# Two changes to a two-block transformer kernel: the order of the last products of each FFN, and a shared weighted sum for the late modulation

## The chip, the cores and the metric

The kernel runs on one core of a Trainium2 chip. Its engines are TensorE (PE, matmuls; PEld is its loading of weights), VectorE (DVE), ScalarE (ACT), GpSimd (POOL) and SyncE (SP, which only issues DMAs here). The metric is the device time of one execution in microseconds. The kernel before takes 3024.43 us (median of 3 runs, 3019.88 to 3027.5). Lower is better.

## The reference

Two transformer blocks with 512 tokens and 1024 channels, all in float32. Two parts matter here. The first is the modulation of the first block (adaLN): a vector `mod` of 6 x 1024 numbers is computed from the condition `c`, and the last four sixths of it are needed only after the first mixer (the "late" part):

```
mod = jax.nn.silu(c) @ w_ada[l] + b_ada[l]
sh1, sc1, gt1, sh2, sc2, gt2 = [m[:, None, :] for m in jnp.split(mod, 6, axis=-1)]
...
x = x + gt1 * mixed
h2 = rms_norm(x, g_norm2[l]) * (1.0 + sc2) + sh2
```

The second is the FFN with a convolution over the tokens, which stands once in each of the two layers of the second block:

```
def _conv_ffn(x, w_up, conv_w, conv_b, w_down):
    g, u = jnp.split(x @ w_up, 2, axis=-1)
    gp = jnp.pad(g, ((0, 0), (half, half), (0, 0)))
    gc = conv_b
    for j in range(FFN_CONV):                    # FFN_CONV = 3
        gc = gc + conv_w[j] * gp[:, j:j + s]
    act = jax.nn.gelu(gc, approximate=False)
    return (act * u) @ w_down                    # inner width 2816
```

## The kernel before, in words

**Data.** Activations are held transposed: 128 channels on the partitions, 512 tokens along the free axis, 8 such tiles (`xT`). Weights come from memory in chunks of up to 128 x 2048 numbers. SyncE loads chunk k into `stage[k % 2]` once chunk k-2 has been split (semaphore `w_split`). ScalarE copies it to a rounded `wH` (line 312), VectorE subtracts to get the rest `wL` (line 317); there are four slots of `wH`/`wL`. Every product of the form weights times activations is three matmuls on TensorE: low x high, high x low, high x high (lines 347, 350, 351).

**The order of work** is written out by hand: each engine has its own program, and semaphores tie them together. Nothing reorders it.

**Late modulation (lines 1057 to 1090 on VectorE, 1745 to 1763 on TensorE).** While the retention of the first mixer is computed in 16 steps w (scores on TensorE, the decay product on VectorE in line 1080, line 1741 on TensorE), each step also handles one 1 MB chunk of `w_ada`, of two halves of 128 x 1024. VectorE multiplies each half by a number per partition and adds it to `ada_sum` (line 1064 for the first of a group, else line 1066). The chunks r and r+2 share a stage buffer: SyncE issues the load of r+2 once r is summed (line 428). After each group of four chunks TensorE sums over the partitions, by 8 matmuls of `ada_sum` with a column of ones (`late_mod`, line 1669 in the helper `mod_cols`; the profile counts 2 passes for each of these float32 matmuls). VectorE may overwrite `ada_sum` only when that is done (line 1059). The fourth result comes before the retention's group norm on TensorE (line 1766). GpSimd has no work in this stretch.

**FFN (lines 1466 to 1522 on VectorE, 814 to 840 on ScalarE, 1991 to 2023 on TensorE).** The inner width is 22 slabs of 128. For slab s TensorE computes the up product (gate and value, 16 x 3 matmuls), VectorE scales, convolves (lines 1495 to 1500), ScalarE applies gelu (line 826), VectorE multiplies (line 1504), ScalarE rounds to `faH` (line 830), VectorE forms `faL` (line 1506). Then TensorE computes the down product of that slab: 8 pieces of 3 matmuls, each into one of 4 PSUM banks in turn, and VectorE adds each piece to `xT` (line 1473) before the bank can be used again. TensorE's order is up(s), down(s-1), for s from 1 to 21, then down(21) alone. After FFN 0 comes the norm `mix1`, after FFN 1 the norm `final2`; each norm is a square on ScalarE (line 531) and a sum over partitions on TensorE (line 1652) for each of the 8 tiles.

## Time and profile before

| What | us |
|---|---|
| median of 3 runs | 3024.43 |
| the profiled execution | 3020.32 |
| its span, first to last instruction | 3018.5 |
| TensorE matmul busy | 2724.8 (90%) |
| VectorE busy | 2260.3 (75%) |
| ScalarE busy | 972.9 (32%) |
| GpSimd busy | 391.2 (13%) |

The late modulation lies between 220 and 295 us of the span, FFN 0 from about 1905 to 2272 us and FFN 1 from about 2635 to 2997 us. A row of a timeline gives the start, the duration, the engine, the line of the kernel, the operation, output <- inputs, the shape and the count; in brackets, how long the engine was idle before it and what released it. "issue" there means that the profile shows nothing that was waited for. PEclk, or the clock, is the share of the full TensorE clock (2.4 GHz) that was granted; 0.50 is 1.2 GHz.

### The profile page before, as it was taken

What the parts mean: (1) busy time and instruction counts of PE and PEld (TensorE: products, weight loads), DVE (VectorE), ACT (ScalarE), POOL (GpSimd) and SP (SyncE); (2) the same over time, 40 slices, a digit from 0 to 9 for tenths busy, and PEclk for the clock granted to TensorE, in tenths of its full rate; (3) what the DMA queues carried; (4) which work ended last, traced back from release to release, by engine and by line L of the source; (5) the groups of instructions that cost most, each with busy time, mean ns of one, the idle gap of its engine ahead of it and who ended that gap; (6) DMA issues with size and microseconds to landing.
All of it is one profiled execution on the core that took longest, in us unless ns stands there. A gap on an engine that the chain in (4) does not pass through costs nothing.

```text
span 3018.5 us, 38456 instructions
## 1 busy us (share of the span) xinstructions
PE 2724.8 (90%) x13529; PEld 2317.3 (77%) x13529; DVE 2260.3 (75%) x3559; ACT 972.9 (32%) x1266; POOL 391.2 (13%) x275
## 2 busy tenths in 40 slices
PE   2976778997999999899999994999999987999997
PEld 1763346897999999899999992788877842788885
DVE  5447755999899977688888877778776465478876
ACT  3220343343344433333333322222223254322221
POOL 0000100012222235333333330000000000000000
PEclk7986799999999999999999997999999998999998
DMA  5216001246788889889999981123222200122221
GB/s 207 91 49 240 32 15 58 84 156 230 245 300 301 299 322 380 326 314 346 347 345 350 344 291 37 65 89 104 87 94 84 98 15 1 49 100 95 99 88 56
DMA packets 158887, 515.47 MB, mean 171 GB/s; under 512 B 11729, under 2 KB 77649, under 8 KB 127057
## 3 DMA queue, kind: packets, MB, share of 16 engines
q1 hardware_dynamic: 109696, 326.62, 30.9%
q0 software_dynamic: 36864, 134.23, 12.2%
q10 hardware_dynamic: 12240, 53.48, 4.4%
q8 instruction: 52, 0.85, 0.1%
q14 instruction: 35, 0.28, 0.0%
HBM read 461.86 MB, written 52.43 MB: 170 GB/s over the span
## 4 chain that ended last, share of the span: by engine, by line
PE 74%; DVE 17%; DMA 4%; ACT 2%; issue 2%; POOL 0%; SPq 0%; ACTq 0%; DVEq 0%
PE ps L347 21%; PE ps L351 21%; PE ps L350 21%; PE ps L1901 3%; DVE sb_wL L317 2%; PE ps L1652 2%; DMA sb_rows<-u_rows,sb_row_at 1%; PE ps L2083 1%; DVE sb_stats L1576 1%; DMA sb_stage<-w_ada_l 1%; DVE sb_rows L1203 1%; DVE sb_ada_sum L1066 1%; PE ps L1835 1%; PE ps L1669 1%; DMA sb_xT<-x_l 1%
## 5 line engine op out<-in xcount | busy, mean ns | idle before, releaser
L347 PE MATMUL ps<-sb_hL,sb_wH 128*128 128x512 f32 (+1 forms) x2256 | 847.4, 376 | 91.0 <-DVE sb_wL L317 33.5
L351 PE MATMUL ps<-sb_hH,sb_wH 128*128 128x512 f32 (+1 forms) x2256 | 829.2, 368 | 0.0
L350 PE MATMUL ps<-sb_hH,sb_wL 128*128 128x512 f32 (+1 forms) x2256 | 828.6, 367 | 0.0
L317 DVE TENSOR_TENSOR sb_wL<-sb_stage,sb_wH 128x2048 fp32r<-128x2048 f32 (+2 forms) x257 | 539.1, 2099 | 188.4 <-ACT sb_wH L312 187.4
L312 ACT ACTIVATE sb_wH<-sb_stage 128x2048 fp32r<-128x2048 f32 (+2 forms) x257 | 447.4, 1758 | 335.3 <-PE ps L347 192.6
L347 PEld LDWEIGHTS ps<-sb_hL,sb_wH 128*128 128x128 f32 x2256 | 427.9, 190 | 155.3 <-issue 70.5
L350 PEld LDWEIGHTS ps<-sb_hH,sb_wL 128*128 128x128 f32 x2256 | 428.1, 190 | 54.1 <-issue 5.8
L351 PEld LDWEIGHTS ps<-sb_hH,sb_wH 128*128 128x128 f32 x2256 | 427.3, 189 | 51.1
L347 PE MATMUL ps<-sb_waL,sb_wH 128*128 128x384 f32 x1024 | 347.2, 339 | 19.2 <-issue 9.8
L351 PE MATMUL ps<-sb_waH,sb_wH 128*128 128x384 f32 x1024 | 346.6, 338 | 0.0
L350 PE MATMUL ps<-sb_waH,sb_wL 128*128 128x384 f32 x1024 | 346.6, 338 | 0.0
L1635 POOL DMA_INDIRECT sb_rows<-u_rows,sb_row_at x128 | 184.0, 1437 | 740.7 <-DVE sb_rows L1203 381.3
L1473 DVE TENSOR_TENSOR sb_xT<-sb_xT,ps 128x512 f32<-128x512 f32 x352 | 230.7, 683 | 39.3 <-PE ps L351 39.2
L1635 POOL DMA_INDIRECT sb_rows<-v_rows,sb_row_at x128 | 187.2, 1462 | 360.6 <-DVE sb_tok L1210 337.7
L347 PEld LDWEIGHTS ps<-sb_waL,sb_wH 128*128 128x128 f32 x1024 | 194.7, 190 | 20.2 <-DVE sb_waL L1362 10.1
L350 PEld LDWEIGHTS ps<-sb_waH,sb_wL 128*128 128x128 f32 x1024 | 194.6, 190 | 0.0
L351 PEld LDWEIGHTS ps<-sb_waH,sb_wH 128*128 128x128 f32 x1024 | 194.4, 190 | 0.0
L826 ACT ACTIVATE sb_gel<-sb_gcv 128x512 f32<-128x512 f32 x44 | 27.8, 632 | 489.9 <-DVE sb_gcv L1498 489.9
L1203 DVE SCALAR_TENSOR_TENSOR sb_rows<-sb_rows,sb_tok 128x1024 f32<-128x1024 f32 x128 | 152.2, 1219 | 36.8 <-DMA sb_rows<-u_rows,sb_row_at 36.7
L1210 DVE SCALAR_TENSOR_TENSOR sb_tok<-sb_rows,sb_row_act,sb_tok 128x1024 f32<-128x1024 f32 x128 | 164.0, 1281 | 10.9 <-DVE sb_tok L1210 2.3
L347 PE MATMUL ps<-sb_faL,sb_wH 128*128 128x512 f32 x352 | 140.8, 400 | 12.8 <-issue 12.8
L351 PE MATMUL ps<-sb_faH,sb_wH 128*128 128x512 f32 x352 | 139.6, 397 | 0.0
(334 smaller groups left out, 3245.2 us busy)
## 6 DMA issues: line engine op xcount, KB each, us to landing
sb_stage<-u_l SPq DMA_DIRECT2D x64, 1024.0 KB
sb_stage<-v_l SPq DMA_DIRECT2D x64, 1024.0 KB
sb_stage<-up_l SPq DMA_DIRECT2D x44, 1024.0 KB
g_scratch<-sb_ga ACTq DMA_DIRECT2D x64, 384.0 KB
w_scratch<-sb_wst ACTq DMA_DIRECT2D x12, 2048.0 KB, 9.9
sb_wg<-w_scratch SPq DMA_DIRECT2D x32, 768.0 KB
...
```

The source lines that it names most:

```text
L312: act.activation(wH[k % SLOTS][:, 0:n], stage[k % STAGES][:, 0:n], ACT.Copy).then_inc(w_hi, 1)
L317: dve.tensor_tensor(wL[k % SLOTS][:, 0:n], stage[k % STAGES][:, 0:n], wH[k % SLOTS][:, 0:n], ALU.subtract).then_inc(w_split, 1)
L347: m = pe.matmul(dst, lh, rl, start=first, stop=False)
L350: pe.matmul(dst, ll, rh, start=False, stop=False)
L351: return pe.matmul(dst, lh, rh, start=False, stop=last)
L1066: op = dve.scalar_tensor_tensor(ada_sum[:, :], w, sc[:, k:k + 1], ada_sum[:, :], ALU.mult, ALU.add)
L1203: dve.scalar_tensor_tensor(rows[r % 4][:, :], rows[r % 4][:, :], 1.0, tok[:, :], ALU.mult, ALU.mult, accum_out=column(row_act, r, i, per)) ...
L1210: dve.scalar_tensor_tensor(tok[:, :], rows[r % 4][:, :], column(row_act, r, i, per), tok[:, :], ALU.mult, ALU.add).then_inc(s_g["used"], 1)
L1473: dve.tensor_tensor(xT[:, d, :], xT[:, d, :], ps[:, 4 + d % 4, :], ALU.add).then_inc(s["added"], 1)
L1635: pool.indirect_dma_start(rows[r % 4][:, :], None, A["u_rows" if r < ROUNDS else "v_rows"], bass.IndirectOffsetOnAxis(ap=row_at[:, r % ROU ...
L1652: pe.matmul(ps[:, norm_bank(name), :], tab[:, ONES, :], scr[:, k % 2, :], start=k == 0, stop=k == nkt - 1).then_inc(s["sum"], 1)
L1901: m = pe.matmul(ps[:, 4 + g0 % 4, q * P:(q + 1) * P], oneJ[g0 % 4][:, q, :], oneI[g0 % 4][:, q, :], start=True, stop=True)
```

## The change

**Late modulation.** VectorE now handles only the first half of each chunk, into `ada_sum[0]`: one instruction in place of two. GpSimd handles the second half, into `ada_sum[1]`. From the second chunk of a group on it does so in two instructions: the half is multiplied in place, and then added. TensorE reduces both sums, with two matmuls per column in place of one. The load of chunk r+2 waits for both engines. Lines of the changed kernel are up to 50 higher.

What VectorE has in a row at the start of the loop, before:

```order
L1066 SCALAR_TENSOR_TENSOR sb_ada_sum<-sb_stage,sb_small,sb_ada_sum 128x1024 [waits ada_summed]
L1080 TENSOR_TENSOR sb_scr<-ps,sb_decay 128x384 [waits ret_ld0,ret_scores,ada_summed]
...
L1066 SCALAR_TENSOR_TENSOR sb_ada_sum<-sb_stage,sb_small,sb_ada_sum 128x1024 [waits ld_ada1]
L1066 SCALAR_TENSOR_TENSOR sb_ada_sum<-sb_stage,sb_small,sb_ada_sum 128x1024 [waits ada_summed]
L1080 TENSOR_TENSOR sb_scr<-ps,sb_decay 128x256 [waits ret_scores,ret_ld0,ret_y,ada_summed]
```

And after, on VectorE:

```order
L1090 TENSOR_TENSOR sb_scr<-ps,sb_decay 128x384 [waits ret_ld0,ret_scores,ada_summed]
L1090 TENSOR_TENSOR sb_scr<-ps,sb_decay 128x384 [waits ret_ld1,ret_scores]
L1076 SCALAR_TENSOR_TENSOR sb_ada_sum<-sb_stage,sb_small,sb_ada_sum 128x1024 [waits ld_ada1]
L1090 TENSOR_TENSOR sb_scr<-ps,sb_decay 128x256 [waits ret_scores,ret_ld0,ret_y,ada_summed]
L1090 TENSOR_TENSOR sb_scr<-ps,sb_decay 128x256 [waits ret_ld1,ret_scores]
```

The second `ada_sum` instruction of each chunk is gone there. GpSimd, which had nothing before its first `hL` subtraction, now has 28 instructions ahead of it, of which the first five are (the first of each group waits for TensorE's reduction of the group before, semaphore `ada_cols`; `ada_sum3` is `ada_sum[1]`):

```order
L1652 TENSOR_SCALAR sb_ada_sum3<-sb_stage0,sb_small 128x1024 [waits ada_cols,ld_ada0]
L1654 TENSOR_SCALAR sb_stage1<-sb_stage1,sb_small 128x1024 [waits ld_ada1,ada_halved]
L1656 TENSOR_TENSOR sb_ada_sum3<-sb_ada_sum3,sb_stage1 128x1024 [waits ada_bit]
L1654 TENSOR_SCALAR sb_stage0<-sb_stage0,sb_small 128x1024 [waits ld_ada0,ada_halved]
L1656 TENSOR_TENSOR sb_ada_sum3<-sb_ada_sum3,sb_stage0 128x1024 [waits ada_bit]
```

Each chunk but the first of a group costs GpSimd two instructions, the second waiting for the first. TensorE at the first `late_mod`, before:

```order
L1756 MATMUL ps<-sb_qk 128x512 [waits ret_decayed]
L1756 MATMUL ps<-sb_qk 128x512
L1669 MATMUL ps<-sb_tab,sb_ada_sum 128x1 [waits ada_summed]
L1669 MATMUL ps<-sb_tab,sb_ada_sum 128x1 x7
L1741 MATMUL ps<-sb_scr,sb_rv 64x128 [waits ret_decayed]
```

And after:

```order
L1797 MATMUL ps<-sb_qk 128x512 [waits ret_decayed]
L1797 MATMUL ps<-sb_qk 128x512
L1787 MATMUL ps<-sb_tab,sb_ada_sum 128x1 [waits ada_halved,ada_summed]
L1787 MATMUL ps<-sb_tab,sb_ada_sum 128x1 x15
L1777 MATMUL ps<-sb_scr,sb_rv 64x128 [waits ret_decayed]
```

The place is the same, with 16 matmuls in place of 8.

**End of each FFN.** The last two up products stand in a row, and the last three down products after them: up(20), up(21), down(19), down(20), down(21), where before it was up(20), down(19), up(21), down(20), down(21). The loads of the weights follow the same order. VectorE's additions of down(19) are put between the operations of slab 21's convolution, and all those of down(20) and down(21) follow it. The end of FFN 0 on VectorE before (L317 splits weights, L1473 adds a piece, L1495 to L1506 are a slab's convolution and activation):

```order
L1473 TENSOR_TENSOR sb_xT<-sb_xT,ps 128x512 [waits ffn0_l_added,ffn0_l_o] x8
L1495 TENSOR_TENSOR sb_graw<-ps,sb_scr 128x512 [waits ffn0_l_proj]
L1496 TENSOR_SCALAR sb_gcv<-sb_graw,sb_vec 128x512 [waits v_chain]
L1497 SCALAR_TENSOR_TENSOR sb_gcv<-sb_graw,sb_vec,sb_gcv 128x511 [waits v_chain]
L1498 SCALAR_TENSOR_TENSOR sb_gcv<-sb_graw,sb_vec,sb_gcv 128x511 [waits v_chain]
L1500 TENSOR_TENSOR sb_uraw<-ps,sb_scr 128x512
L1504 TENSOR_TENSOR sb_fa<-sb_gel,sb_uraw 128x512 [waits ffn0_l_lo,ffn0_l_gelu,v_chain]
L1506 TENSOR_TENSOR sb_faL<-sb_fa,sb_faH 128x512 [waits ffn0_l_hi]
L1473 TENSOR_TENSOR sb_xT<-sb_xT,ps 128x512 [waits ffn0_l_added,ffn0_l_o] x8
```

And after (L1481 is the addition):

```order
L1505 TENSOR_TENSOR sb_graw<-ps,sb_scr 128x512 [waits ffn_proj]
L1506 TENSOR_SCALAR sb_gcv<-sb_graw,sb_vec 128x512 [waits v_chain]
L1481 TENSOR_TENSOR sb_xT<-sb_xT,ps 128x512 [waits ffn_added,ffn_o,v_chain]
L1509 SCALAR_TENSOR_TENSOR sb_gcv<-sb_graw,sb_vec,sb_gcv 128x511
L1481 TENSOR_TENSOR sb_xT<-sb_xT,ps 128x512 [waits ffn_added,ffn_o,v_chain]
L1512 SCALAR_TENSOR_TENSOR sb_gcv<-sb_graw,sb_vec,sb_gcv 128x511
L1514 TENSOR_TENSOR sb_uraw<-ps,sb_scr 128x512
L1481 TENSOR_TENSOR sb_xT<-sb_xT,ps 128x512 [waits ffn_added,ffn_o,v_chain]
L1520 TENSOR_TENSOR sb_fa<-sb_gel,sb_uraw 128x512 [waits ffn_lo,ffn_gelu]
L1481 TENSOR_TENSOR sb_xT<-sb_xT,ps 128x512 [waits ffn_added,ffn_o] x5
L1525 TENSOR_TENSOR sb_faL<-sb_fa,sb_faH 128x512 [waits ffn_hi]
L1481 TENSOR_TENSOR sb_xT<-sb_xT,ps 128x512 [waits ffn_added,ffn_o] x16
```

Before, 8 additions stand behind the last slab's chain; now 24 stand within and behind it. The loops run one iteration less and two slabs more are written out; the two FFNs share one set of semaphores with offsets (`f_at`).

The core of the diff:

```diff
@@ VectorE, late modulation @@
-                for j in range(2):
-                    k = 2 * (r % 4) + j
-                    w = stage[r % 2][:, j * D:(j + 1) * D]
-                    ...
-                    op.then_inc(s_ada["summed"], 1)
-                    dve.wait_ge(s_ada["summed"], KT + 2 * r + j + 1)
+                k = 2 * (r % 4)
+                w = stage[r % 2][:, 0:D]
+                ...
+                op.then_inc(s_ada["summed"], 1)
+                dve.wait_ge(s_ada["summed"], KT + r + 1)
@@ GpSimd @@
+            for r in range(16):
+                pool.wait_ge(ld_ada[r % 2], 16 * (KT // 4 + r // 2 + 1))
+                if r % 4 == 0:
+                    pool.wait_ge(s_ada["cols"], 1 + r // 4)
+                k = 2 * (r % 4) + 1
+                w = stage[r % 2][:, D:2 * D]
+                if k == 1:
+                    pool.tensor_scalar(ada_sum[1][:, :], w, sc[:, 1:2], None, ALU.mult).then_inc(s_ada["halved"], 1)
+                else:
+                    pool.tensor_scalar(w, w, sc[:, k:k + 1], None, ALU.mult).then_inc(s_ada["bit"], 1)
+                    pool.wait_ge(s_ada["bit"], r - r // 4)
+                    pool.tensor_tensor(ada_sum[1][:, :], ada_sum[1][:, :], w, ALU.add).then_inc(s_ada["halved"], 1)
+                pool.wait_ge(s_ada["halved"], r + 1)
@@ TensorE, late_mod @@
-                mod_cols(3, 16 + 8 * g, ada_sum, 8)
+                pe.wait_ge(s_ada["halved"], 4 * (g + 1))
+                for f in range(8):
+                    for half in range(2):
+                        m = pe.matmul(ps[:, 3, 16 + 8 * g + f:17 + 8 * g + f], ada_sum[half][:, f * P:(f + 1) * P],
+                                      tab[:, ONES, 0:1], start=half == 0, stop=half == 1)
@@ SyncE @@
-                    sp.wait_ge(s_ada["summed"], KT + 2 * (r - 1))
+                    sp.wait_ge(s_ada["summed"], KT + r - 1)
+                    sp.wait_ge(s_ada["halved"], r - 1)
@@ SyncE, FFN loads @@
+                load(sp, c + 2 * FT - 5, A["up_l"][l, FT - 2])
+                load(sp, c + 2 * FT - 4, A["up_l"][l, FT - 1])
+                for s0 in range(FT - 3, FT):
+                    load(sp, c + FT + s0, A["down_l"][l, s0])
@@ TensorE, FFN @@
-                ffn_pe(l, c, FT - 2)
-                ffn_pe(l, c, FT - 1)
-                ffn_pe(l, c, FT, has_a=False)
+                ffn_pe(l, c, FT - 4)
+                ffn_pe(l, c, FT - 3)
+                ffn_pe(l, c, FT - 2, has_o=False)
+                ffn_pe(l, c, FT - 1, has_o=False, up=2 * FT - 4)
+                for s0 in range(FT - 2, FT + 1):
+                    ffn_pe(l, c, s0, has_a=False, down=FT + s0 - 1)
```

## Rows read from the trace of the kernel before

**Rows 1.** The page, section 4: the chain that ended last, by engine.

```profile
PE 74%; DVE 17%; DMA 4%; ACT 2%; issue 2%; POOL 0%; SPq 0%; ACTq 0%; DVEq 0%
```

**Rows 2.** Timeline of VectorE, 225 to 261 us (late modulation).

```profile
225.12 0.75 DVE L1064 TENSOR_SCALAR sb_ada_sum<-sb_stage,sb_small 128x1024 f32<-128x1024 f32 x1 [2.52 <-DMA sb_stage<-w_ada_l]
...
235.84 2.60 DVE L1066 SCALAR_TENSOR_TENSOR sb_ada_sum<-sb_stage,sb_small,sb_ada_sum 128x1024 f32<-128x1024 f32 x2 [0.60 <-DMA sb_stage<-w_ada_l]
...
242.19 0.75 DVE L1064 TENSOR_SCALAR sb_ada_sum<-sb_stage,sb_small 128x1024 f32<-128x1024 f32 x1 [2.42 <-PE ps L1669]
...
244.30 1.22 DVE L1086 TENSOR_TENSOR sb_rg<-sb_rg,sb_scr 128x1024 f32<-128x1024 f32 x1
245.44 1.01 DVE L1080 TENSOR_TENSOR sb_scr<-ps,sb_rope_r 128x384 f32<-128x384 f32 x2
...
253.77 2.60 DVE L1066 SCALAR_TENSOR_TENSOR sb_ada_sum<-sb_stage,sb_small,sb_ada_sum 128x1024 f32<-128x1024 f32 x2 [0.68 <-DMA sb_stage<-w_ada_l]
...
260.11 0.75 DVE L1064 TENSOR_SCALAR sb_ada_sum<-sb_stage,sb_small 128x1024 f32<-128x1024 f32 x1 [2.41 <-PE ps L1669]
```

**Rows 3.** Timeline of TensorE: first and last of four late reductions, and what follows.

```profile
238.50 3.58 PE L1669 MATMUL ps<-sb_tab,sb_ada_sum 128*128 128x1 f32 x16 [3.57 <-DVE sb_ada_sum L1066]
...
291.44 3.57 PE L1669 MATMUL ps<-sb_tab,sb_ada_sum 128*128 128x1 f32 x16 [2.77 <-DVE sb_ada_sum L1066]
294.87 5.71 PE L1766 MATMUL ps<-sb_qk,sb_tab 128*128 128x512 f32 x8
```

**Rows 4.** DMA issues between 220 and 300 us: kind, count, size, microseconds to landing.

```profile
sb_stage<-w_ada_l SPq DMA_DIRECT2D x16, 1024.0 KB, 4.9
```

**Rows 5.** TensorE in the first modulation: length, busy (passes), granted clock, DMA share, GB/s.

```profile
46.00:53.00 7.00, 6.99 (x32) 0.50 0.00 0
```

**Rows 6.** By line, minimum/median/maximum ns: GpSimd's subtractions, and VectorE's copies beside them.

```profile
L1625 POOL TENSOR_TENSOR sb_hL<-sb_qk,sb_hH x4: 1275/1278/1287, 315.4 to 320.5; 128x512 fp32r<-128x512 f32 x4
L1619 POOL TENSOR_TENSOR sb_qnL<-sb_lat,sb_qnH x2: 1437/1594/1752, 322.6 to 324.3; 128x512 fp32r<-128x512 f32 x2
L1122 DVE COPY sb_kh<-sb_lat x8: 409/411/1476, 323.2 to 328.7; 32x512 f32<-32x512 f32 x8
```

**Rows 7.** Timeline of TensorE: from up(20) of FFN 0, and FFN 1's last product.

```profile
2223.99 0.40 PE L347 MATMUL ps<-sb_hL,sb_wH 128*128 128x512 f32 x1
...
2256.64 0.40 PE L351 MATMUL ps<-sb_faH,sb_wH 128*128 128x512 f32 x1
...
2263.45 0.77 PE L347 MATMUL ps<-sb_faL,sb_wH 128*128 128x512 f32 x1 [6.41 <-issue]
...
2987.97 0.76 PE L347 MATMUL ps<-sb_faL,sb_wH 128*128 128x512 f32 x1 [6.41 <-issue]
```

**Rows 8.** TensorE, the end of FFN 0, columns as in rows 5.

```profile
2257.10:2263.40 6.30, 0.00 (x0) 0.86 0.00 0
2263.50:2268.00 4.50, 4.50 (x11) 0.50 0.00 0
2268.50:2271.30 2.80, 2.80 (x13) 1.00 0.00 0
```

**Rows 9.** Timeline of VectorE, the end of FFN 0.

```profile
2252.27 5.50 DVE L1473 TENSOR_TENSOR sb_xT<-sb_xT,ps 128x512 f32<-128x512 f32 x8 [3.09 <-PE ps L351]
2257.68 0.68 DVE L1495 TENSOR_TENSOR sb_graw<-ps,sb_scr 128x512 f32<-128x512 f32 x1
...
2258.98 0.75 DVE L1497 SCALAR_TENSOR_TENSOR sb_gcv<-sb_graw,sb_vec,sb_gcv 128x511 f32<-128x511 f32 x1
...
2262.66 0.69 DVE L1506 TENSOR_TENSOR sb_faL<-sb_fa,sb_faH 128x512 fp32r<-128x512 f32 x1 [0.69 <-ACT sb_faH L830]
...
2268.80 3.44 DVE L1473 TENSOR_TENSOR sb_xT<-sb_xT,ps 128x512 f32<-128x512 f32 x5 [0.45 <-PE ps L351]
```

**Rows 10.** Timeline of TensorE behind FFN 0: norm sums, next product.

```profile
2271.35 8.59 PE L1652 MATMUL ps<-sb_scr,sb_tab 128*128 128x512 f32 x16
2279.38 0.80 PE L347 MATMUL ps<-sb_hL,sb_wH 128*128 128x512 f32 x1
```

115 lines of the change are left out of this document (66 added, 49 removed).

## The prediction

> **What bounds the kernel now.** I read the page's chain first [rows 1]: three quarters of it are TensorE, 17% VectorE, 4% DMA, and no share is GpSimd's. So a change counts only where TensorE waits, and the change touches two such places, each read in the timelines of VectorE and TensorE.
>
> *Late modulation, 220 to 295 us.* A group of four chunks takes 260.11 - 242.19 = 17.92 us [rows 2]. The reader is to see what ends each wait: the group's last chunk starts when its DMA lands (253.77), VectorE needs 2.60 us for its two halves, TensorE 3.58 us for 16 passes [rows 3], and VectorE may only then begin the next group (the 2.4 us waits on PE). The last chunk's load was issued when the second chunk was summed, 4.9 us earlier [rows 4]. So the group's period is a loop of first chunk, second chunk, a load of 4.9, the last chunk, the reduction. The retention fits beside it. The last reduction ends at 291.44 + 3.57 = 295.01, and TensorE goes on with the group norm at once [rows 3]: whatever this stretch gains or loses, the kernel does.
>
> *The end of each FFN.* TensorE runs without a gap from up(20) at 2223.99 to the end of down(20) at 2257.04, 144 matmuls, 0.228 us from start to start, so 10.97 us for an up product and 5.5 for a down product. Then it stands still for 6.41 us, in both FFNs alike [rows 7]. VectorE explains it: it adds down(20) until 2257.7, works through slab 21's chain until 2263.35, and only then can down(21) start [rows 9]. In the gap the granted clock falls; the first 4.5 us of down(21) run at 0.50, that is 1.2 GHz, and the rest at 2.4 GHz [rows 8]. Down(21) so takes 2271.35 - 2263.45 = 7.9 us in place of 5.5.
>
> **Late modulation, part by part.** Removed: the second of VectorE's two instructions per chunk, 16 of 1.3 us. Added: 28 instructions on GpSimd, and 8 matmuls (16 passes) in each of four reductions.
>
> *The reductions.* 32 passes stand in the trace: the first modulation, 6.99 us, at clock 0.50 throughout [rows 5]. So each late one goes from 3.58 to 7.0 us, +3.4. A reduction and what precedes it are serial, so nothing covers it; GpSimd now waits for it too. The Trainium skill ("TensorE: Matmul & The Clock Gate", the part on the HAM clock gate) says that activity releases the throttle; by that alone the second half of 7 us would be faster, but the 32 passes of the row stayed at 1.2 GHz, so the measurement decides.
>
> *GpSimd.* The trace shows no multiplication by a column on it. It shows subtractions of two 128x512 inputs, 1.28 us undisturbed and 1.44 to 1.75 beside VectorE [rows 6]. An addition of 128x1024 is then estimated at 2 x 1.28 = 2.56 us; its ends are VectorE's multiply-and-add of that width, 1.28 (2.60 for two, [rows 2]), and 2 x 1.75 = 3.5. The multiplication reads one input, so as many numbers as the 128x512 subtraction: 1.28 us, its ends VectorE's 0.75 [rows 2] and the full 2.56. With 0.15 us for the hand-over between them and disturbance, a chunk costs 4.0 us, a group's first chunk 1.3.
>
> *The sum.* Chunk 0 lands at 225.1 [rows 2] and is done at 226.4; chunk 1 at 230.5; chunk 2 lands at 231.3 (226.4 + 4.9) and is done at 235.3; chunk 3 lands at 235.4 and is done at 239.4 (before: 238.44); the reduction ends at 246.45 (before: 242.1). A group from there: first chunk 1.3; second done at 5.35; third lands at 6.2, done at 10.2; fourth lands at 5.35 + 4.9 = 10.3, done at 14.3; reduction until 21.35, and 0.05 to start, so 21.4 in place of 17.92. VectorE's half of the second chunk ends at about 4.5 even behind line 1086 (1.22) and line 1080 (1.01) and is hidden. The groups start at 246.5, 267.9 and 289.3, the last reduction ends at 310.6: **+15.6 us**. Half of it is the passes, half that GpSimd takes 4.0 us where VectorE took 2.6; the load of 4.9 stays in the loop. Behind the waiting GpSimd instruction stand only the subtractions due at 315 us and later, behind VectorE's wait the decay products, which have several microseconds of room, and behind SyncE's the loads of `w_out`, wanted after the attention.
>
> *Ends.* With the fast ends (0.75 and 1.28) VectorE's 4.5 us becomes the second chunk's end, the group takes 18.7, the last reduction ends at 298.5: +3.5. With the slow ends (2.56 and 3.5, so 6.2 us a chunk) a group takes 28.3 and it is +43. I take 15.6, since the GpSimd rows are nearer than VectorE's. The skill's "GPSIMD Engine Reference" (sections on performance versus the vector engine and on engine selection) speaks against this change: a two-input operation is about half as fast as on VectorE, 4497 ns for 2048 numbers, a one-input one at line rate. By it an estimate is 2.25 us for the addition and 1.0 for the multiplication, 3.4 us a chunk, and the sum would be about +9.6. Rows 6 agree on the factor of two, and are a little slower.
>
> **End of the FFNs, step by step.** With up(20) at 0, up(21) ends at 22.0 and down(19) starts at once: its inputs were ready long before. Slab 19's chain, 5.7 us long as slab 21's in rows 9, and slab 20's lie beside up(20) and up(21), 11 us each, with room for the splits between them. The 6.41 us gap goes, and down(21) no longer starts cold. What is late next is VectorE: at 22.0 it has slab 21's seven instructions and all 24 additions left. The seven are 0.55 to 0.75 us, 4.8 together; the additions are 5.50 / 8 = 0.687 us [rows 9], 16.5 together. That is 21.3 plus 0.1, so it ends at 43.4, where before it ended at 2268.80 + 3.44 - 2223.99 = 48.25. TensorE has only 16.5 us of work there and is held by the four banks: piece 6 of down(19) waits some 1.4 us for the third addition, piece 7 and piece 4 of down(20) 0.7 each, and from there on it runs at VectorE's pace. The last piece ends at about 41.6; before it was 2271.35 - 2223.99 = 47.36. So TensorE gains 5.8 and VectorE 4.8. Which counts? Behind FFN 0, TensorE goes straight on with the norm sums, paced by ScalarE's squares from the end of its products, 2271.35 to 2279.4 [rows 10]; VectorE needs 4.5 us of splits and 0.7 per `hL` tile first, so its tile 0 is ready at 48.7 of my count while TensorE asks for it at 49.6. Behind FFN 1 the squares are paced by TensorE's sums too. So **-5.8 us in each, -11.6**.
>
> *Ends.* At most: no stall at all, 6.41 and the 2.4 of the cold start, -8.8 each, -17.6. At least: the new stalls lower the clock once per FFN and give 2.0 us back, -7.6. ScalarE's `faH` of slab 21 waits for down(19) to end, since both use one buffer; that is at 29.8, and VectorE wants it at 31.8 behind its additions, so it costs nothing; behind it on ScalarE stand only the next stage's splits, wanted at 43.
>
> The other edits (shared semaphores, two slabs written out) cost nothing: TensorE has no gap in the loop that a shorter loop could close.
>
> **Sum.** +15.6 - 11.6 = +4.0. The profiled execution took 3020.3 (span 3018.5), which gives 3024.3 for it. That execution lies 4.1 below the median of the runs, 3024.4, against which the change is timed: **3028.4 us**. What can't be told from no change is 0.3%, 9 us.
>
> **The rivals.**
>
> *A: GpSimd is the bound in earnest.* Its multiplication costs as much as its addition, 2.56, or the shared access to the memory slows both; VectorE's copies went from 0.41 up to 1.48 us beside GpSimd [rows 6]. At 5.3 us per chunk it never waits for a load: chunks end at 227.7, 233.0, 238.3, 243.6, a group is 2.6 + 3 x 5.3 + 7.05 = 25.6, the last reduction ends at 327.4, +32.4. Net +20.8: 3045. It decides (slower by 9 us) from about 4.6 us per chunk. Against it: one input in place of two.
>
> *B: the modulation costs little and the FFN ends give all.* GpSimd at VectorE's rate, and TensorE not held by the banks: +3.5 - 17.6, 3010. Against it: rows 6, and 24 additions of 0.687, which no order makes shorter.
>
> *C: the FFN ends give less.* The stalls of the three down products lower the clock: +15.6 - 7.6 = +8.0, 3032.4. For it: the clock fell within a gap of 6.3 us [rows 8]; against it: the new waits are 1.4 us and less.
>
> That the change doesn't do what it says I rule out: TensorE's and GpSimd's programs have the new instructions in the new places.
>
> **How the numbers follow.** Forecast 0.58, A 0.25, C 0.12, B 0.05. Faster by over 0.3%: B and 0.03 of the forecast's lower end, where GpSimd takes 3 us per chunk and the FFNs give over 8 each, 0.08. Slower by over 0.3%: most of A, under half of C and a little of the forecast, 0.31. The rest, 0.61, within 0.3%. The range goes from 3018 (3.4 us per chunk and 8 us per FFN, net -6.4) to 3044, just short of A's price.
>
> **What would show it.** Right: 32-pass reductions of 7.0 us, the last ending near 310.6; GpSimd rows of about 1.3 and 2.6 us; loads still 4.9; no TensorE wait over 2 us between up(20) and the norm sums, and 41 to 42 us from the start of up(20) to the end of down(21). Wrong: a multiplication on GpSimd over 2 us (A); reductions well under 7 us; the last reduction before 303; a granted clock under 1 in the three down products (C); any wait of TensorE for weights there.

## The result and the profile after

The changed kernel takes 3050.84 us (median; 3048.27 to 3055.35), the kernel before 3024.61 on the same chip: ratio 1.0094, 95% interval 1.0075 to 1.0114: slower by 0.9%, and the interval lies clear of 1. The profiled execution's span is 3050.7 us against 3018.5. The forecast was 3028.4 with a range up to 3044, so the time lies outside, above it.

The page of the changed kernel, section 4, the chain that ended last, by engine (compare [rows 1]):

```profile
PE 73%; DVE 16%; POOL 3%; DMA 3%; ACT 2%; issue 2%; SPq 0%; ACTq 0%; DVEq 0%; POOLq 0%
```

GpSimd had no share of the chain, now it has 3%. To see where the time went I use three lengths that can be read from any of these traces: the *loop* (start of VectorE's first decay product to the start of the addition that ends the late modulation), and each *FFN* (start of VectorE's first gate product to the start of its last addition into `xT`). What lies between loop and FFN 0 differs from execution to execution, kernels with the same code there included, by up to 9 us (1613 to 1622 us), so single spans can't tell a few microseconds; the three lengths and the ratios can.

| kernel | loop, us | FFN 0, us | FFN 1, us |
|---|---|---|---|
| before | 73.8 | 359.6 | 359.1 |
| changed | 118.7 | 352.9 | 352.7 |

So the late modulation costs +44.9 us, and the FFNs give back 6.7 and 6.4. Sum +31.8; the spans differ by 32.2.

**Late modulation.** Timeline of GpSimd, changed kernel, the second of four groups and the start of the third (start us, duration us; a bracket is idle time before and what ended it; L1652 and L1654 multiply by the column, L1656 adds):

```profile
254.60 3.37 POOL L1652 TENSOR_SCALAR sb_ada_sum<-sb_stage,sb_small 128x1024 f32<-128x1024 f32 x1 [7.30 <-PE ps L1787]
258.06 2.84 POOL L1654 TENSOR_SCALAR sb_stage<-sb_stage,sb_small 128x1024 f32<-128x1024 f32 x1
260.99 2.35 POOL L1656 TENSOR_TENSOR sb_ada_sum<-sb_ada_sum,sb_stage 128x1024 f32<-128x1024 f32 x1
263.44 3.69 POOL L1654 TENSOR_SCALAR sb_stage<-sb_stage,sb_small 128x1024 f32<-128x1024 f32 x1
267.21 2.34 POOL L1656 TENSOR_TENSOR sb_ada_sum<-sb_ada_sum,sb_stage 128x1024 f32<-128x1024 f32 x1
...
283.06 3.37 POOL L1652 TENSOR_SCALAR sb_ada_sum<-sb_stage,sb_small 128x1024 f32<-128x1024 f32 x1 [7.30 <-PE ps L1787]
```

The reader is to see that between two brackets GpSimd never waits: within a group it is the bound. A group takes 283.06 - 254.60 = 28.46 us (17.92 before, 21.4 forecast). The addition, 2.34, is what was forecast (2.56) or better. The multiplication is 2.84 to 3.69 where the forecast had 1.28 and its slow end 2.56: a chunk costs 6.2 us, not 4.0. The loads still land 4.9 us after their issue, and none of them is waited for within a group.

Timeline of TensorE, the reductions of the first group and of the last (answer to [rows 3]):

```profile
247.44 6.96 PE L1787 MATMUL ps<-sb_tab,sb_ada_sum 128*128 128x1 f32 x32 [13.73 <-POOL sb_ada_sum L1656]
...
333.66 6.96 PE L1787 MATMUL ps<-sb_tab,sb_ada_sum 128*128 128x1 f32 x32 [10.22 <-POOL sb_ada_sum L1656]
```

6.96 us, forecast 7.0; but TensorE waits 10 to 14 us for GpSimd before each. The stretch of the first of them (length, TensorE busy, weight load busy, VectorE, ScalarE, GpSimd, granted clock, DMA share, GB/s) stayed at 0.50, as in [rows 5]:

```profile
247.50:254.30 6.80, 6.80 (x32) 6.80 (x32) 0.00 (x0) 0.00 (x0) 0.00 (x0) 0.50 0.48 157
254.60:275.90 21.30, 7.62 (x32) 2.29 (x31) 11.59 (x13) 1.65 (x2) 20.62 (x7) 0.66 0.49 173
```

The second line is the stretch between two reductions: GpSimd is busy 20.62 of 21.30 us, VectorE 11.59. VectorE's rows of the same group (answer to [rows 2]):

```profile
254.51 0.75 DVE L1074 TENSOR_SCALAR sb_ada_sum<-sb_stage,sb_small 128x1024 f32<-128x1024 f32 x1 [11.02 <-PE ps L1787]
255.29 2.02 DVE L1096 TENSOR_TENSOR sb_rg<-sb_rg,sb_scr 128x1024 f32<-128x1024 f32 x1
...
258.17 2.08 DVE L1076 SCALAR_TENSOR_TENSOR sb_ada_sum<-sb_stage,sb_small,sb_ada_sum 128x1024 f32<-128x1024 f32 x1
...
263.10 1.32 DVE L1076 SCALAR_TENSOR_TENSOR sb_ada_sum<-sb_stage,sb_small,sb_ada_sum 128x1024 f32<-128x1024 f32 x1 [2.05 <-DMA sb_stage<-w_ada_l]
...
268.51 2.12 DVE L1076 SCALAR_TENSOR_TENSOR sb_ada_sum<-sb_stage,sb_small,sb_ada_sum 128x1024 f32<-128x1024 f32 x1 [3.57 <-DMA sb_stage<-w_ada_l]
```

Read these beside GpSimd's. In each of these pairs the operation that starts second, while the other engine's is running, is the long one, here by about 0.8 us: L1096, 2.02 in place of 1.22 in [rows 2], starts within GpSimd's 254.60; L1076 at 258.17, 2.08 in place of 1.3, starts just behind GpSimd's 258.06, which stays at 2.84; at 263.10 VectorE is first and stays at 1.32, and GpSimd's multiplication at 263.44 takes 3.69; at 268.51 VectorE starts within GpSimd's addition of 267.21 and takes 2.12. Not every operation is stretched: the decay products (L1090), which take one input from PSUM, keep the length that they had before, 1.01 us at 257.24 as at 245.44 in [rows 2], though GpSimd is at work.

**End of an FFN.** Timeline of VectorE, changed kernel, end of FFN 0 (answer to [rows 9]; L1505 is the first instruction of slab 21's chain, L1481 the additions):

```profile
2292.21 0.69 DVE L1505 TENSOR_TENSOR sb_graw<-ps,sb_scr 128x512 f32<-128x512 f32 x1 [3.70 <-PE ps L356]
2292.94 0.55 DVE L1506 TENSOR_SCALAR sb_gcv<-sb_graw,sb_vec 128x512 f32<-128x512 f32 x1
2293.52 0.69 DVE L1481 TENSOR_TENSOR sb_xT<-sb_xT,ps 128x512 f32<-128x512 f32 x1
...
2298.09 3.07 DVE L1481 TENSOR_TENSOR sb_xT<-sb_xT,ps 128x512 f32<-128x512 f32 x5
2301.08 0.69 DVE L1525 TENSOR_TENSOR sb_faL<-sb_fa,sb_faH 128x512 fp32r<-128x512 f32 x1
2301.68 10.13 DVE L1481 TENSOR_TENSOR sb_xT<-sb_xT,ps 128x512 f32<-128x512 f32 x16
```

TensorE's two waits in that stretch (answer to the 6.41 us of [rows 7]):

```profile
2297.63 0.50 PE L352 MATMUL ps<-sb_faL,sb_wH 128*128 128x512 f32 x1 [1.02 <-DVE sb_xT L1481]
...
2298.83 0.51 PE L352 MATMUL ps<-sb_faL,sb_wH 128*128 128x512 f32 x1 [0.23 <-DVE sb_xT L1481]
```

VectorE is never idle from slab 21's chain on, TensorE waits 1.25 us in all, and in the columns of the windows above the stretch stays at the full clock, where [rows 8] had 0.86 and 0.50:

```profile
2292.20:2297.60 5.40, 4.39 (x18) 2.93 (x17) 5.25 (x9) 0.63 (x1) 0.00 (x0) 1.00 0.09 36
2297.60:2299.10 1.50, 1.24 (x4) 0.76 (x5) 1.50 (x3) 0.00 (x0) 0.00 (x0) 1.00 0.00 0
2299.10:2311.80 12.70, 12.70 (x54) 9.73 (x54) 12.66 (x22) 6.62 (x7) 0.00 (x0) 1.00 0.01 2
```

### The profile page after: what moved, and what is told of

It is laid out like the page before. It is cut to its first block, busy times and chain, and to the rows that moved or that the text cites. A ratio compares the mean times of both kernels' runs of the same rounds, so it can differ in the third digit from the quotient of the medians.

```text
span 3050.7 us, 38467 instructions
## 1 busy us (share of the span) xinstructions
PE 2735.4 (90%) x13593; PEld 2324.9 (76%) x13593; DVE 2247.0 (74%) x3543; ACT 972.3 (32%) x1266; POOL 464.4 (15%) x303
## 4 chain that ended last, share of the span: by engine, by line
PE 73%; DVE 16%; POOL 3%; DMA 3%; ACT 2%; issue 2%; SPq 0%; ACTq 0%; DVEq 0%; POOLq 0%
PE ps L352 21%; PE ps L356 21%; PE ps L355 21%; PE ps L1942 3%; DVE sb_wL L322 2%; PE ps L1688 2%; POOL sb_stage L1654 1%; DMA sb_rows<-u_rows,sb_row_at 1%; PE ps L2127 1%; POOL sb_ada_sum L1656 1%; PE ps L1787 1%; DVE sb_stats L1598 1%; PE ps L1876 1%; DVE sb_rows L1213 1%; DMA sb_xT<-x_l 1%
## 5 line engine op out<-in xcount | busy, mean ns | idle before, releaser
L317 ACT ACTIVATE sb_wH<-sb_stage 128x2048 fp32r<-128x2048 f32 (+2 forms) x257 | 447.2, 1757 | 336.5 <-PE ps L352 185.4
L1671 POOL DMA_INDIRECT sb_rows<-u_rows,sb_row_at x128 | 174.4, 1362 | 750.3 <-DVE sb_rows L1213 387.6
L1481 DVE TENSOR_TENSOR sb_xT<-sb_xT,ps 128x512 f32<-128x512 f32 x352 | 228.8, 684 | 27.4 <-PE ps L356 27.1
```

Of the source, the lines that this page charges most:

```text
L317: act.activation(wH[k % SLOTS][:, 0:n], stage[k % STAGES][:, 0:n], ACT.Copy).then_inc(w_hi, 1)
L1481: dve.tensor_tensor(xT[:, d, :], xT[:, d, :], ps[:, 4 + d % 4, :], ALU.add).then_inc(s["added"], 1)
L1671: pool.indirect_dma_start(rows[r % 4][:, :], None, A["u_rows" if r < ROUNDS else "v_rows"], bass.IndirectOffsetOnAxis(ap=row_at[:, r % ROU ...
```

## The experiments

Theory 1: the loss is the late modulation alone, and in it GpSimd's multiplication, whose form is slow by itself and slower beside VectorE; the FFN ends give their 6.5 us each whatever stands ahead of them. Rivals: the doubled passes, or the loads, are what costs; contention alone is what costs; the two changes lean on each other. All ratios are to the kernel before, on the same chip, with 95% intervals. What each kernel measured:

| kernel | time, us | ratio | interval | loop | FFN 0 | FFN 1 |
|---|---|---|---|---|---|---|
| changed | 3050.8 | 1.0094 | 1.0075 to 1.0114 | 118.7 | 352.9 | 352.7 |
| only the FFN change | 3007.6 | 0.9957 | 0.9941 to 0.9973 | 74.7 | 352.8 | 352.7 |
| only the FFN change, run again | 3010.5 | 0.9953 | 0.9939 to 0.9967 | 74.6 | 352.8 | 352.7 |
| only the late modulation's change | 3064.3 | 1.0143 | 1.0128 to 1.0157 | 119.7 | 359.0 | 358.9 |
| two sums on VectorE | 3019.4 | 0.9992 | 0.9981 to 1.0003 | 86.0 | 353.0 | 352.8 |
| GpSimd's product with two inputs | 3040.2 | 1.0063 | 1.0046 to 1.0080 | 107.7 | 352.8 | 352.7 |
| GpSimd without multiplication | 3022.5 | 1.0002 | 0.9993 to 1.0012 | 89.6 | 352.8 | 352.8 |
| additions first | 3018.1 | 0.9979 | 0.9969 to 0.9989 | 74.7 | 356.6 | 357.6 |
| additions later | 3009.8 | 0.9957 | 0.9946 to 0.9969 | 74.5 | 354.9 | 354.6 |
| two sum buffers | 3007.4 | 0.9954 | 0.9940 to 0.9968 | 73.1 | 352.8 | 352.7 |
| and half loads | 3005.5 | 0.9947 | 0.9933 to 0.9961 | 73.2 | 352.8 | 352.7 |
| and the reduction later | 3001.2 | 0.9920 | 0.9906 to 0.9933 | 66.0 | 352.8 | 352.8 |

The last five, and the one with two sums on VectorE, have only the FFN change beside what their names say, and the late modulation on VectorE.

### Each change alone

Only the FFN change (the late modulation as before):

```diff
-                w = stage[r % 2][:, 0:D]
+                for j in range(2):
+                    w = stage[r % 2][:, j * D:(j + 1) * D]
...
-                    pool.tensor_scalar(w, w, sc[:, k:k + 1], None, ALU.mult).then_inc(s_ada["bit"], 1)
-                    pool.wait_ge(s_ada["bit"], r - r // 4)
-                    pool.tensor_tensor(ada_sum[1][:, :], ada_sum[1][:, :], w, ALU.add).then_inc(s_ada["halved"], 1)
```

> Only the order at the end of both FFNs is changed; the late modulation is as before (VectorE forms the whole sum, 8 matmuls a reduction). Theory 1 (the late modulation's four groups cost 45 us in the changed kernel, the two FFN ends give back 6.6 and 6.9, and nothing couples them): the span falls by 13.5 us, to about 3011, with both FFN ends as early as in the changed kernel. Rival (part of what the FFN ends seemed to give back was made up by the lateness of everything ahead of them, such as a DMA that had come in earlier by then): the span falls by less than 10 us.

Measured: 3007.6 us, ratio 0.9957, about 13 us less than before; loop 74.7, FFNs 352.8 and 352.7. Run a second time beside the last kernel of this section:

> The kernel with only the FFN change once more, beside the one before it in this list on the same chip, so that a few us between them can be told. Loop 74 to 75 us, each FFN 352.8 us, ratio to before 0.9957 within 0.0015 (theory 1 and rival alike).

Measured: 3010.5 us, ratio 0.9953 (0.9939 to 0.9967), as expected. Only the late modulation's change (the diff of before with the FFN lines left out; it uses an existing semaphore for GpSimd's steps):

> Only the late modulation is changed (GpSimd forms the second half, 16 matmuls a reduction); the FFNs are as before. Theory 1 (the two changes add up): the loop with the late modulation, from its first decay to the modulation's bias, 118 to 120 us against 73.8, each FFN 359 us as before, and in all +40 to +46 us. Rival (some of the lateness is taken up behind the modulation, which the changed kernel hides since its FFNs are shorter): less than +38 us.

Measured: ratio 1.0143, about 43 us more; loop 119.7, FFNs 359.0 and 358.9, and TensorE's 6.4 us gap is back. The ratios add up: 0.0143 - 0.0043 = 0.0100 against the 0.0094 of both together, within the intervals. No coupling between the two changes shows within the intervals; theory 1 holds.

### The passes without GpSimd

```diff
-                    if k == 0:
+                    if k < 2:
-                        op = dve.tensor_scalar(ada_sum[:, :], w, sc[:, 0:1], None, ALU.mult)
+                        op = dve.tensor_scalar(ada_sum[j][:, :], w, sc[:, k:k + 1], None, ALU.mult)
...
+                    for half in range(2):
+                        m = pe.matmul(..., ada_sum[half][:, f * P:(f + 1) * P], tab[:, ONES, 0:1], start=half == 0, stop=half == 1)
```

> FFN ends as in the changed kernel; VectorE alone forms both halves, in two sums, and TensorE adds them with 16 matmuls a group (32 passes). GpSimd has no part. Theory 1 (the price of the late modulation in the changed kernel is GpSimd's, 6.2 us a chunk, and the passes alone add 3.4 us a group): against the kernel with only the FFN change +3.4 us for each of four groups, less about 0.5 us a group for a plain multiplication in place of a multiplication with addition: +11 to +14 us, so the span is about 3023 (near the kernel before). Rival (the doubled passes are what costs, by a clock or a queue that the trace hides): +25 us or more against it.

Measured: loop 86.0, +11.3 against the FFN change alone; 3019.4 us, +11.8. The first reduction of this kernel:

```profile
238.19 6.98 PE L1771 MATMUL ps<-sb_tab,sb_ada_sum 128*128 128x1 f32 x32 [3.63 <-DVE sb_ada_sum L1075]
```

So of the 44.9 us the passes are some 11, and GpSimd's part is the other 33 (118.7 - 86.0). The 11.3 hold the half microsecond that a plain multiplication in place of one with addition saves in each group; the reductions alone are 3.4 us longer, 13.5 in four. The rival would have needed 25.

### GpSimd's multiplication in another form

```diff
-                    pool.tensor_scalar(w, w, sc[:, k:k + 1], None, ALU.mult)
+                    pool.tensor_tensor(w, w, sc[:, k:k + 1].broadcast_to([P, D]), ALU.mult)
```

> The changed kernel with one edit: GpSimd multiplies the chunk by the column as an operation of two inputs (the column repeated along the row by a stride of zero), not as one by a scalar of each partition. Theory 1 (what is slow is the form: the scalar form took 3.4 to 3.7 us for 128x1024, the two-input addition of the same size 2.34): each multiplication takes about 2.34 us, a chunk 4.7 to 4.8 instead of 6.2, a group 5.9 us less, all four about 22 us less than the changed kernel, so about 3028. Rival (the multiplication is slow because it runs while VectorE and the DMA work on the same tile, and the additions are quick because they run when VectorE waits): the multiplications stay at 3.3 us or above in this form too, and the time within 5 us of the changed kernel's.

Measured: loop 107.7, 11.0 less than the changed kernel's, where 22 was expected; the rival expected less than 5. GpSimd's first three instructions of a group, and a chunk of the last group:

```profile
250.03 2.44 POOL L1652 TENSOR_TENSOR sb_ada_sum<-sb_stage,sb_small 128x1024 f32<-128x1024 f32 x1 [7.27 <-PE ps L1787]
252.54 2.76 POOL L1654 TENSOR_TENSOR sb_stage<-sb_stage,sb_small 128x1024 f32<-128x1024 f32 x1
255.38 3.21 POOL L1656 TENSOR_TENSOR sb_ada_sum<-sb_ada_sum,sb_stage 128x1024 f32<-128x1024 f32 x1
...
305.21 1.89 POOL L1654 TENSOR_TENSOR sb_stage<-sb_stage,sb_small 128x1024 f32<-128x1024 f32 x1
307.18 3.21 POOL L1656 TENSOR_TENSOR sb_ada_sum<-sb_ada_sum,sb_stage 128x1024 f32<-128x1024 f32 x1
```

The form counts, but neither theory had the sizes: the same multiplication takes 1.89 us where it starts ahead of VectorE's operation and 2.76 where it starts within it, and an addition can be the one that starts second, too (3.21). Half of the expected gain was so lost to contention, which had been left out of the expectation. The operation had to be measured by itself.

### The operations by themselves

```diff
+            for phase in range(3):
+                for n, f in enumerate(KINDS):
+                    f(pool, X, Y, sc).then_inc(pb_p, 1)
```

> The kernel with only the FFN change, and after its last norm a series of operations of 128x1024 float32 on the free weight buffers, which leave the results alone: on GpSimd a multiplication by a column out of place, the same in place, a multiplication by a number, an addition of two inputs, a multiplication with the column repeated along the row, and a copy, twice each; first with VectorE still, then beside a stream of VectorE's multiplications with addition (scalar_tensor_tensor), then beside a stream of its multiplications by a column (tensor_scalar). Theory 1 (the form of one scalar for each partition is what costs): 3.3 us or above for the column forms with VectorE still, 2.3 for the two-input forms. Rival (contention with VectorE or with the loads stretched it): the column form takes about 1.3 to 2.3 us with VectorE still and 3.4 or more only beside a stream; then VectorE's own operations beside it are the longer ones too. For VectorE itself: its multiplication with addition took 1.28 us before and 2.08 to 2.32 beside GpSimd, so in the second phase above 2 us.

One execution, 3132 us. GpSimd's timeline with VectorE still (two of each, so half of the duration is one; L88 by a column, L92 the same in place, L96 by a number, L100 addition, L104 product with the repeated column, L108 copy), then three lines from beside VectorE's stream of multiplications with addition:

```profile
3017.02 5.80 POOL L88 TENSOR_SCALAR sb_stage<-sb_stage,sb_small 128x1024 f32<-128x1024 f32 x2 [443.92 <-DVE sb_stage L1670]
3022.91 5.78 POOL L92 TENSOR_SCALAR sb_stage<-sb_stage,sb_small 128x1024 f32<-128x1024 f32 x2
3028.78 5.62 POOL L96 TENSOR_SCALAR sb_stage<-sb_stage 128x1024 f32<-128x1024 f32 x2
3034.49 4.75 POOL L100 TENSOR_TENSOR sb_stage<-sb_stage 128x1024 f32<-128x1024 f32 x2
3039.32 3.87 POOL L104 TENSOR_TENSOR sb_stage<-sb_stage,sb_small 128x1024 f32<-128x1024 f32 x2
3043.25 2.14 POOL L108 COPY sb_stage<-sb_stage 128x1024 f32<-128x1024 f32 x2
...
3054.28 6.66 POOL L92 TENSOR_SCALAR sb_stage<-sb_stage,sb_small 128x1024 f32<-128x1024 f32 x2
...
3067.61 6.06 POOL L100 TENSOR_TENSOR sb_stage<-sb_stage 128x1024 f32<-128x1024 f32 x2
3073.75 5.59 POOL L104 TENSOR_TENSOR sb_stage<-sb_stage,sb_small 128x1024 f32<-128x1024 f32 x2
```

Undisturbed, GpSimd's multiplication by a scalar takes 2.9 us, by a column or by a number (2.8), in place or not; the two-input addition 2.37, the product with a repeated column 1.94, the copy 1.07 (each is half of a pair and holds the short hand-over; one addition by itself is 2.34). So the form costs: with one full input it is slower than with two. The expectation (3.3 or above) was too high by the contention: beside this stream of VectorE the multiplication in place, the addition and the product with the repeated column are 3.3, 3.0 and 2.8, and beside the other stream, VectorE's multiplications by a column, GpSimd's multiplication takes up to 3.8. VectorE pays too:

```profile
3010.54 3.93 DVE L1665 SCALAR_TENSOR_TENSOR sb_stage<-sb_stage,sb_small 128x1024 f32<-128x1024 f32 x3
...
3045.50 44.15 DVE L1665 SCALAR_TENSOR_TENSOR sb_stage<-sb_stage,sb_small 128x1024 f32<-128x1024 f32 x24 [28.67 <-POOL sb_stage L108]
```

3.93 / 3 = 1.31 us alone, 44.15 / 24 = 1.84 in the stream, whose last few ran when GpSimd was done; of the 19 beside GpSimd the median is 1.94 and the longest 3.24. In the changed kernel, then, a multiplication of 3.69 is 2.9 of its own and 0.8 of contention. Both theories held a part.

The copy is at the rate that the Trainium skill ("GPSIMD Engine Reference", the section on engine selection) gives one-input operations, near line rate, and the addition near the 2.25 us that is estimated as half of the page's 4497 ns for 2048 numbers; a multiplication by a scalar has one input too and is at neither.

How late the second of two operations is can be read from the pairs, by the profile's rather rough GpSimd times. In most it is what the first has left to run, less 0.1 to 0.2 us. At 263.44 VectorE's operation has 0.98 us left, and GpSimd's takes 0.85 more than the 2.84 of 258.06. At 268.51 GpSimd's addition has 1.04 left, and VectorE's takes 0.84 more than its 1.28. The exception is GpSimd's multiplication by a scalar when it is first: at 255.29 and at 258.17 it has 2.7 us left, and VectorE's operation is only 0.80 late and ends before it (258.17 + 2.08 = 260.25, GpSimd's ran until 260.90). So 0.8 us is not a fixed price of an overlap; the delay can be longer, as the next kernel shows.

The Trainium skill's "SBUF — State Buffer" ("Who interferes with whom") says that GpSimd and a VectorE operation with two inputs in the memory contend for a pair of ports that is an exclusive lock; of VectorE's two-port modes it says that whoever issues first has the pair for the whole instruction and the other fully blocks. The pairs above agree with both, but for those behind GpSimd's multiplication by a scalar, where VectorE was late by 0.80 us and not by 2.7.

### GpSimd without the multiplication

```diff
-                    pool.tensor_scalar(ada_sum[1][:, :], w, sc[:, 1:2], None, ALU.mult).then_inc(s_ada["halved"], 1)
+                    pool.tensor_copy(ada_sum[1][:, :], w).then_inc(s_ada["halved"], 1)
...
-                    pool.tensor_scalar(w, w, sc[:, k:k + 1], None, ALU.mult).then_inc(s_ada["bit"], 1)
-                    pool.wait_ge(s_ada["bit"], r - r // 4)
```

> The changed kernel without GpSimd's multiplications: it copies the first chunk of a group and adds the others unweighted (so the late modulation's values are not the reference's; nothing else is left out). Theory 1 (the multiplication, 3.4 to 3.7 us where the forecast had 1.28, is the whole of the miss; what is left on GpSimd, one operation of about 2.4 us a chunk, is below the pace of the loads): the loop goes by the loads and the 32 passes, 85 to 89 us as with both sums on VectorE (86.0), against 118.7, and the time is 30 to 34 us under the changed kernel's, at a ratio to before of 0.999 to 1.001. Rival (something else of GpSimd's share costs as well: its waits, its place in the chain, what it does to VectorE and the loads): the loop stays above 95 us and the ratio above 1.002.

Measured: loop 89.6 (a little over the 89 expected), ratio 1.0002. GpSimd now waits for loads within a group:

```profile
252.63 3.38 POOL L1654 TENSOR_TENSOR sb_ada_sum<-sb_ada_sum,sb_stage 128x1024 f32<-128x1024 f32 x1 [1.94 <-DMA sb_stage<-w_ada_l]
256.61 3.38 POOL L1654 TENSOR_TENSOR sb_ada_sum<-sb_ada_sum,sb_stage 128x1024 f32<-128x1024 f32 x1 [0.61 <-DMA sb_stage<-w_ada_l]
```

The time is 28 us under the changed kernel's (3050.8 against 3022.5), where 30 to 34 were expected; the rival, a loop above 95 us, is out. So the loop is 118.7 - 89.6 = 29.1 us shorter without the multiplications, and the forecast's late modulation was short by 44.9 - 15.6 = 29.3. The agreement is in part chance: this kernel has no multiplication at all, where the forecast had one of 1.28 us a chunk, and its loop waits for loads, where the changed kernel's waits for GpSimd. A multiplication of 1.28 us was not run.

The addition of 3.38 is worth a look: 2.34 when it follows a multiplication, it now starts 0.1 us behind VectorE's operation and pays 1.0. It can be worse the other way round. VectorE in the first group of this kernel:

```profile
230.58 3.26 DVE L1076 SCALAR_TENSOR_TENSOR sb_ada_sum<-sb_stage,sb_small,sb_ada_sum 128x1024 f32<-128x1024 f32 x1
```

It starts 0.17 us behind GpSimd's addition of 230.41 (2.35 us long, so 2.18 left) and takes 1.98 more than its 1.28.

### The end of the FFNs in another order

All eight additions of down(19) ahead of slab 21's chain:

```diff
+                if adds:
+                    for d in range(KT):
+                        ffn_add(l, adds, d)
```

> The kernel with only the FFN change, but at the end of each FFN VectorE makes all eight additions of the last slab but one ahead of the last slab's subtractions, not one after each. Theory 1 (the end is VectorE's sum of work, 24 additions and the chain of the last slab, in whatever order): within 1.5 us of the kernel with only the FFN change for each FFN. Rival (the interleaving is what keeps TensorE fed: the last slab's activations reach it later by the eight additions, 8 x 0.6 us, and its last matmuls end later by that): 3 to 5 us later at each FFN, 6 to 10 in all.

Measured: +3.8 and +4.9 us per FFN, 3018.1 us. VectorE has the same work and waits more: 5.3 us on TensorE, most of it for the first piece of down(19), where it waited 3.7 for slab 21's gate product, and once for ScalarE's `faH` of slab 21 (the other 0.7 is slab 20's, as ever):

```profile
DVE sb_xT L1480 <- PE ps L356: 5.3, 3, 4.4
DVE sb_faL L1527 <- ACT sb_faH L838: 1.4, 2, 0.7
```

TensorE then waits too. Its four banks hold the first four pieces of down(20), and VectorE's additions of these now stand behind slab 21's chain: TensorE is idle for 4.21 us, until the first of them is done at 2263.2, and behind that wait the granted clock is 0.50 (2264.5 to 2266.5) and 1.00 again from 2267.5.

The rival's size holds. Its reason, that the last slab's activations come later, is not what ends TensorE's long wait; the bank is. The forecast called this end "24 additions of 0.687, which no order makes shorter"; that is not so: this order of the same work makes the end 4 to 5 us longer than the change's. The other way round, the additions behind the chain's product:

```diff
-                    if beside:
-                        beside(0)
...
-                        for d in range(3, KT):
+                        for d in range(KT):
```

> The kernel with only the FFN change, with VectorE's eight additions of the last slab but one behind the product of the last slab's activation, not three of them between its steps. With all eight ahead of the chain an FFN took 3.8 to 4.9 us more (356.6 and 357.6 against 352.8 and 352.7 us from its first gate to its last addition). Theory 1 (what counts is how early the last slab's activation is done, since TensorE waits for it): 0 to 2 us less for each FFN, since the product comes three additions, 1.8 us, sooner. Rival (TensorE's banks come free by these additions, so they are as urgent as the chain): 1 to 3 us more for each FFN, with TensorE waiting for VectorE's additions longer than the 1.2 us that it does now. Second rival (VectorE's sum of work alone): within 0.5 us of it.

Measured: 354.9 and 354.6, +2.1 and +1.9 per FFN: its rival. TensorE's waits of this kernel between slab 21's start and the end:

```profile
PE ps L352 <- DVE sb_xT L1480: 2.2, 1, 2.2
```

It was 1.2 with the additions between the steps, in two waits of which the longer is 1.0. Behind the wait of 2.2 us the clock fell here too: seven matmuls in a row take 0.63 us and start 0.43 apart, where the others take 0.40 and start 0.23 apart, some 1.4 us in all. The longer wait (+1.0) and the clock (+1.4) together are near the +2.1. With the additions between the steps no wait of TensorE was followed by the lower clock. By the lengths of the FFNs the order that the change has is the best of the three; between this one and the change's the time does not show it (3009.8 against 3007.6, on two chips).

### What bounds the loop without GpSimd

```diff
-                if r % 4 == 0 and r:
-                    dve.wait_ge(s_ada["cols"], 1 + r // 4)
+                if r % 4 == 0 and r >= 8:
+                    dve.wait_ge(s_ada["cols"], r // 4)
...
-                        op = dve.tensor_scalar(ada_sum[:, :], w, sc[:, 0:1], None, ALU.mult)
+                        op = dve.tensor_scalar(ada_sum[r // 4 % 2][:, :], w, sc[:, 0:1], None, ALU.mult)
```

> The kernel with only the FFN change, and VectorE's sum of each group goes to the other of two buffers, so that it does not wait for TensorE to have read the one before. VectorE waited 2.42 us for it in each of three groups. Theory 1 (that wait is on the path): 5 to 7.3 us less than the kernel with only the FFN change. Rival (the load of the next chunk, 5.1 us to landing into a buffer that came free late, takes its place): less than 2 us.

Loop 73.1 against 74.7: the rival's. Half loads on top:

```diff
-                sp.dma_start(stage[r % 2][:, :], A["w_ada_l"][KT + r])
+                    sp.dma_start(stage[r % 2][:, j * D:(j + 1) * D], A["w_ada_l"][KT + r][:, j * D:(j + 1) * D])
```

> The kernel with two sum buffers, and each chunk of the late modulation's weights is loaded as two halves, each issued when VectorE has read that half of the buffer. With two sum buffers alone the loop took 73.1 us against 74.7. Theory 1 (the loop waits for loads: landing 5.1 us and 2.6 us of sums for each of two buffers, about 4 us a chunk, so the sums of VectorE or GpSimd were never the limit): each half is issued 1.3 us sooner, and the loop is 5 to 10 us shorter. Rival (what limits is VectorE, with 2.6 us of sums and 0.9 us of decays a chunk and the waits between its own steps, or the loads move no faster in halves): less than 2 us.

73.2, nothing. What VectorE waited for in the loop, with the FFN change alone, and then with half loads (us in total, times, longest):

```profile
DVE sb_ada_sum L1073 <- PE ps L1690: 7.3, 3, 2.4
DVE sb_ada_sum L1075 <- DMA sb_stage<-w_ada_l: 4.7, 7, 1.1
DVE sb_ada_sum L1073 <- DMA sb_stage<-w_ada_l: 2.6, 1, 2.6
```

```profile
DVE sb_ada_sum L1077 <- DMA sb_stage<-w_ada_l: 4.8, 6, 1.9
DVE sb_scr L1091 <- PE ps L1779: 3.7, 2, 2.3
DVE sb_ada_sum L1075 <- DMA sb_stage<-w_ada_l: 2.3, 2, 2.0
```

The wait for the reduction went, and a wait for scores (L1779) came, 5.2 us with the two sum buffers alone and 3.7 with half loads: TensorE makes them behind the reduction, and stands there waiting for VectorE's sum. So:

```diff
-                if w >= 4 and w % 4 == 0:
-                    late_mod(w // 4 - 1)
                 if w >= 1:
                     ret_y(w - 1)
+                if w >= 4 and w % 4 == 1:
+                    late_mod(w // 4 - 1)
```

> The kernel with two sum buffers and half loads, and TensorE makes the reduction of a group one window of the retention later (behind that window's scores and the products of the one before). With half loads VectorE waited in the loop 7.1 us for loads and 3.7 us for scores, which stood behind a reduction for which TensorE waited up to 5.5 us for VectorE's sum. Theory 1 (TensorE's order, scores behind the reduction, is what took the place of the waits that the two sum buffers removed): the 3.7 us go and the loads start sooner, the loop takes 66 to 71 us against 73.1, the time 2 to 7 us under the one with only the FFN change. Rival (the loads set the pace by themselves): within 1.5 us of 73.1.

Loop 66.0, 3001.2 us, ratio 0.9920 (0.9906 to 0.9933): theory 1. The wait for scores in the loop is down to 0.2:

```profile
DVE sb_ada_sum L1077 <- DMA sb_stage<-w_ada_l: 4.8, 9, 0.9
...
DVE sb_scr L1091 <- PE ps L1779: 0.2, 1, 0.2
```

This kernel is faster than both, than the one before by 22 us. On the same chip it is 9.3 us under the one with only the FFN change (3001.2 against 3010.5), more than the 2 to 7 expected; the loops differ by 8.6. Whether it needs the half loads, or the two sum buffers, was not run.

## Why the prediction was wrong

**The step that failed** is in *GpSimd*: "The multiplication reads one input, so as many numbers as the 128x512 subtraction: 1.28 us, its ends VectorE's 0.75 and the full 2.56." The mechanism around it was right, a serial chain of GpSimd and the reduction; this term of the sum was mis-sized: 2.9 us undisturbed, 3.4 to 3.7 in three or four of a group's four chunks. It was sized by the count of numbers read. The rows had no operation of that form on GpSimd, so nothing but an analogy stood behind either the value or its end. With it a chunk took 6.2 us, and at that pace GpSimd waits for no load, where the sum had the load of 4.9 in the loop. The 6.2 is just what the slow end of the addition (3.5) and of the multiplication (2.56) made together with the hand-over, by two errors that cancel; from it the text had "+43", and measured is +44.9. That this end came so near is luck. Yet the range stopped at 3044, just short of rival A's price, though A had a chance of 0.25.

**What came is rival A**, priced at 5.3 us a chunk and +32.4 us, with the point from which it decides at 4.6. Its sign that was named, a multiplication of over 2 us, is what the trace shows. It was given 0.25 on the argument "one input in place of two", which the operations by themselves refute.

**Contention** was put at 0.15 us a chunk with the hand-over. For the multiplication alone it was 0.5 to 0.85, in three or four of a group's four chunks, since both engines start at about the same landing. [Rows 6] showed contention (0.41 to 1.48 for a copy, 1.75 for a subtraction of 1.28) and only the slow end of the sum took it in.

**The share of the passes** was misread in the forecast's own sum. It says that of the 15.6 us half is the passes and half that GpSimd takes 4.0 us for 2.6. But a group grew by 3.5 us in it (17.92 to 21.4), of which 3.4 are the passes, so 13.6 of the 15.6 in four groups: GpSimd's slower last chunk was made up by an earlier second one. Measured, with both sums on VectorE, the passes came to 11.3.

**Right in the late modulation:** the reductions, 6.96 against 7.0; the addition, 2.34 against 2.56; the landing time, 4.9 us as before. The estimate from the Trainium skill's "GPSIMD Engine Reference", 3.4 us a chunk, missed by more than the forecast's 4.0, in the same direction.

**The FFN ends:** the mechanism held step by step, the gap of 6.41 gone, 1.2 us of waits for additions (forecast 2.8), no cold start, nothing slower by the clock (C is out for this order, though the two other orders show its mechanism), TensorE's last piece done 40.7 us after the start of up(20), where 41.6 was forecast, and VectorE's last addition 41.6, where it was 43.4. They gave 6.7 and 6.4, not 5.8, for the most part because 16 additions in a row take 10.13 us, 0.63 each, not 0.687. The 0.687 (5.50 / 8 in [rows 9]) is TensorE's pace, three matmuls of 0.229 a piece, and not what an addition costs where VectorE is the one behind. What the forecast had wrong there is the reason: the end is not VectorE's sum of work in any order.

**The other side:** without the slow term the forecast's balance may have come out. The kernel without the multiplications is at 1.0002, where the forecast was 1.0013; but it leaves out the whole term and not only the excess, so this is argued and not shown.
